# One transfer and one split per weight slot in a two-layer GLA and retention trunk

## The chip, the cores and the metric

The kernel runs on one core of one Trainium2 chip. The metric is the device time of one launch in microseconds (us). TensorE is called PE, VectorE DVE, ScalarE ACT, GpSimd POOL, SyncE SP.

## What is computed

Two layers over 2048 prompt tokens (width 1024) and over 8 single decode tokens that carry their own states. Cut to what matters:

```
def _layer(x, pos, s_gla, s_ret, norm_w, w_in, gla_w2, gla_b, ..., w_out, chunked):
    h = _rmsnorm(x, norm_w)
    z = jnp.einsum('btd,dc->btc', h, w_in).astype(F32)
    gq, gk, gv, gg, glr, rq, rk, rv, rg = _split_cols(z)
    ...
    o_a, s_gla_new = _gla_chunked(q_a, k_a, v_a, la, s_gla)
    o_b, s_ret_new = _ret_chunked(q_b, k_b, v_b, s_ret)
    ...
    mixed = jnp.concatenate([o_a, o_b], axis=-1).astype(x.dtype)
    y = x + jnp.einsum('btc,cd->btd', mixed, w_out)
    return y, s_gla_new, s_ret_new
```

All of it is float32. The two projections, h times w_in (1024 x 3088) and mixed times w_out (1024 x 1024), are most of the arithmetic.

## The kernel before

**Tiling.** The prompt is cut into 4 blocks of 512 tokens, so that 2 layers give 8 blocks, n = 0 to 7. Block b of a layer is number l * 4 + b; the decode tokens go along with the blocks b = 0 and 1 of each layer. In each block the projections are 8 units u, each 512 output columns wide: 0 to 5 from w_in, 6 and 7 from w_out. A unit is 4 slots s, and a slot is 256 rows of the weights as a tile of 128 x 1024 (two halves of 512 columns, one for each 128 rows). So there are 32 slots per block and 256 in all; w = 4u + s + 1 counts the steps of a block. Weights are read again from memory in every block.

**The split product.** A float32 product is made of three rounded ones (L754): a weight half is rounded into `w_hi` (type fp32r), the remainder goes into `w_lo`; the activations are split in the same way into `h_hi`, `h_lo` (units 0 to 5) and `m_hi`, `m_lo` (units 6 and 7). A slot is 4 banks q times 2 halves times 3 products, 24 matmuls.

**The path of a weight half.** h counts the halves (2 per slot).

- `load_half` (L244 to L258), issued from ACT's queue, brings 128 x 512 floats, 256 KB, into a staging buffer: `w_stage`, or parts of `ss` and `v_b`, which hold the decode states at other times. It waits for the last reader of that buffer. Each half has one of four semaphores `w_loaded`.
- `split_hi` (L260 to L267) on ACT waits for the load and, with the first half of a slot, for `slot_used`: the slot three before has been used by PE (RING is 3). It writes `w_hi` and raises `hi_done`.
- `split_lo` (L269 to L274) on POOL waits for `hi_done`, subtracts, writes `w_lo` and raises `lo_done`. PE waits for `lo_done` of both halves (L799 `unit_slot`), only the first slot of the program waits for each by itself (L784 `first_slot`).

In step w, ACT splits the slot w + 1 steps on and issues the load of the one behind it, half by half:

```
for h in (2 * (w + AHEAD - 1), 2 * (w + AHEAD - 1) + 1) if w > 0 else ():
    split_hi(act, n * HALVES + h)
    load_half(act, n * HALVES + h + 2)
```

**Order.** Each engine's order of work is written out by hand, step by step, and every engine works strictly in that order; semaphores tie the engines together. Around the change, these share an engine with it or stand behind it:

- ACT: `next_hi` (L366) writes `h_hi` of the next block in steps 28 to 31, right behind the step's splits; L1104 empties the low-rank product that PE's `gate_expand` (L780) needs; L1170 empties the attention outputs; the first activation of the program loads a table.
- DVE: `next_scaled` (L398) scales the next block's rows with a factor in a PSUM bank; `next_lo` (L370) writes `h_lo` from `x_t` (in the tile `xn`) and `h_hi`, both in SBUF; in step 29 four L1685 add the banks of unit 6 to the residual rows, which frees the banks for unit 7 (`free_bank` on PE). L1511 is a normalisation, L1325 updates the decode states, which PE's L873 reads.
- POOL: besides `split_lo` small powers (L627) and, at step 23, parts of `m_lo` (L687).
- PE at the start: `scale_rows` with 10 and then 18 idle turns (`idle_turns`, L375), then the first slot, with 8 idle turns behind its first product.
- SP: all other transfers; the rows of block 1 (L423) are loaded when slot 0 has been used.

Of the kernel before, what the change touches and what calls it, by code (L numbers as in the profile page):

```python
# [32 lines left out]
RING = 3  # L33
# [27 lines left out]
def build(nc, d):  # L61
# [3 lines left out]
    with ctx:  # L65
# [105 lines left out]
        w_loaded = [sem(f"w_loaded{r}") for r in range(2 * AHEAD)]  # L171
# [72 lines left out]
        def load_half(act, h):  # L244
            if h >= DEPTH * NBLK * HALVES:
                return
            before = [p for p in range(max(0, h - STAGES), h) if buffer(p) == buffer(h)]
            if before:
                act.wait_ge(lo_done, before[-1] + 1)
                if in_decode(before[-1]) and before[-1] // HALVES % NBLK == 0:  # L250
                    act.wait_ge(z_ps.sem, z_ps.at(before[-1] // HALVES // NBLK, before[-1] % HALVES // 8 + 1))
                elif in_decode(before[-1]):
                    act.wait_ge(slot_used, used(before[-1] // 2 // 4 * 4 + 3))
            elif h >= STAGES:
                act.wait_ge(state_out, h // HALVES // NBLK * 64 + 64)
                act.wait_ge(so_ps.sem, so_ps.at(h // HALVES // NBLK, 2))
            row = h // HALVES // NBLK * (SLOTS - 1) + h % HALVES // 2
            act.dma_start(stage(h), d["w_slots"][row, :, 512 * (h % 2):512 * (h % 2) + 512]).then_inc(w_loaded[h % (2 * AHEAD)], 16)  # L258

        def split_hi(act, h):  # L260
            if h >= DEPTH * NBLK * HALVES:
                return
            act.wait_ge(w_loaded[h % (2 * AHEAD)], (h // (2 * AHEAD) + 1) * 16)
            if h % 2 == 0 and h // 2 >= RING:
                act.wait_ge(slot_used, used(h // 2 - RING))
            c = slice(512 * (h % 2), 512 * (h % 2) + 512)
            nc.scalar.activation(w_hi[:, h // 2 % RING, c], stage(h), ACT.Copy).then_inc(hi_done, 1)  # L267

        def split_lo(pool, h):  # L269
            if h >= DEPTH * NBLK * HALVES:  # L270
                return
            pool.wait_ge(hi_done, h + 1)
            r, c = h // 2 % RING, slice(512 * (h % 2), 512 * (h % 2) + 512)
            pool.tensor_tensor(w_lo[:, r, c], stage(h), w_hi[:, r, c].bitcast(f32), ALU.subtract).then_inc(lo_done, 1)  # L274
# [129 lines left out]
        def _(sp):  # L404
# [109 lines left out]
            for n in range(DEPTH * NBLK):  # L514
# [8 lines left out]
                for w in range(20):  # L523
# [29 lines left out]
                    if b == 1:  # L553
                        if w == 3:
                            sp.wait_ge(lo_done, n * HALVES)
                            load_states(l, "state_ret")
                        if w == 8:
                            sp.wait_ge(stored.sem, stored.at(n, 0))
                            if l == 0:
                                sp.wait_ge(xstat.sem, xstat.at(n + 1, 1))  # L560
                            load_v(l, 0)
                        if w == 9:
                            sp.wait_ge(s_v.sem, s_v.at(l, V_SS[0]))
                            save_states(l, "ret_s")
                            load_v(l, 1)
                            sp.wait_ge(state_out, l * 64 + 32)
                            sp.wait_ge(so_ps.sem, so_ps.at(l, 1))
                            load_states(l, "state_gla")
# [44 lines left out]
        def _(pool):  # L613
# [36 lines left out]
            for h in range(2):  # L650
                split_lo(pool, h)
            for h in range(2, 2 * AHEAD):
                split_lo(pool, h)
# [3 lines left out]
            for l in range(DEPTH):  # L657
                def body(l, n, kind):
                    for w in range(SLOTS):
                        if w > 0:  # L660
                            split_lo(pool, n * HALVES + 2 * (w + AHEAD - 1))
                            split_lo(pool, n * HALVES + 2 * (w + AHEAD - 1) + 1)
# [34 lines left out]
        def _(pe):  # L697
# [10 lines left out]
            for l in range(DEPTH):  # L708
                def body(l, n, kind):
# [48 lines left out]
                    def last_slots():  # L758

                        pe.wait_ge(lo_done, DEPTH * NBLK * HALVES)  # L760
# [23 lines left out]
                    def first_slot():  # L784

                        for k in range(2):
                            pe.wait_ge(lo_done, k + 1)
                            pe.wait_ge(hlo_sb.sem, hlo_sb.at(0, k + 1))
                            products(0, 0, 0, (k,))
                            if k == 0:  # L790
                                idle_turns(pe, 8)
# [7 lines left out]
                    def unit_slot(u, s):  # L799
                        w = 4 * u + s + 1  # L800
                        first = n * HALVES + 2 * (4 * u + s)
                        pe.wait_ge(lo_done, first + 2)
# [231 lines left out]
        def _(act):  # L1034
            act.wait_ge(sets, 7)
            act.wait_ge(x_first[1], 16)
            load_half(act, 0)
            load_half(act, 1)
            act.wait_ge(first_xt[0], 16)
            load_half(act, 2)  # L1040
            load_half(act, 3)
            split_hi(act, 0)
            next_hi(act, 0, 0)
            split_hi(act, 1)
            for k in range(1, KT):
                next_hi(act, 0, k)
                if k == 1:
                    load_half(act, 4)
                    load_half(act, 5)
                if k in (2, 3):  # L1050
                    split_hi(act, k)
            for l in range(DEPTH):
                def body(l, n, kind):
# [45 lines left out]
                    for w in range(SLOTS):  # L1099
# [31 lines left out]
                        for h in (2 * (w + AHEAD - 1), 2 * (w + AHEAD - 1) + 1) if w > 0 else ():  # L1131
                            split_hi(act, n * HALVES + h)
                            load_half(act, n * HALVES + h + 2)
# [724 lines left out]
```

## Time and profile before

| what | value |
|---|---|
| median of 3 runs | 1656.39 us (1655.0 to 1656.63) |
| the profiled execution | 1656.71 us, span 1654.9 us |
| PE busy | 1636.2 us, 99% of the span |
| DVE, ACT, POOL busy | 1065.8, 616.3 and 837.1 us (64%, 37%, 51%) |
| HBM read | 219.34 MB, 161 GB/s with what is written |
| weight loads | 512 of 256 KB (344 to w_stage, 112 to ss, 56 to v_b) |

The table says that PE is nearly always at work and that every other engine has room on average. An average does not tell whether PE waits at a certain place, for that the waits and the timeline are read.

### The profile page before, as it was taken

How to read it: one execution, taken by the hardware profiler on the slowest of the kernel's cores; microseconds unless marked ns; L12 is line 12 of the kernel's file. 1: busy time of each engine (PE TensorE's matmuls, PEld its weight loads, DVE VectorE, ACT ScalarE, POOL GpSimd, SP SyncE). 2: the span in 40 equal slices, each digit the busy share in tenths (PEclk: the TensorE clock that was granted, in tenths of full speed). 3: DMA queues.
4: the chain of work that ended last, by engine and by line, in shares of the span. 5: the costliest groups of instructions: out<-in, count | busy, mean ns of one | idle time of the engine just before them, and what ended most of it. 6: DMA issues, size and time to landing. Idle time of an engine off the chain costs nothing.

```text
span 1654.9 us, 26309 instructions
## 1 busy us (share of the span) xinstructions
PE 1636.2 (99%) x9802; PEld 1353.3 (82%) x9802; DVE 1065.8 (64%) x2372; ACT 616.3 (37%) x1150; POOL 837.1 (51%) x645
## 2 busy tenths in 40 slices
PE   7999999999999999999999999999999999999998
PEld 5888878888888887888878888788888888878887
DVE  6743676678764575547854467757887557784474
ACT  4523434234342343423443234342343324442342
POOL 4543645545455454554544445456555455554455
PEclk9999999999999999999999999999999999999999
DMA  7444656767555564467643656566764377553554
GB/s 273 105 134 149 179 204 167 195 199 212 169 111 148 158 197 135 120 159 161 196 136 108 158 139 197 159 185 185 186 193 140 111 168 162 174 169 102 144 154 141
DMA packets 389135, 268.18 MB, mean 162 GB/s; under 512 B 290704, under 2 KB 293136, under 8 KB 389008
## 3 DMA queue, kind: packets, MB, share of 16 engines
q1 hardware_dynamic: 315136, 131.99, 31.4%
q10 hardware_dynamic: 73872, 134.51, 25.9%
q8 instruction: 77, 1.26, 0.3%
q14 instruction: 50, 0.41, 0.1%
HBM read 219.34 MB, written 47.07 MB: 161 GB/s over the span
## 4 chain that ended last, share of the span: by engine, by line
PE 94%; DMA 2%; DVE 2%; issue 0%; ACT 0%; SPq 0%; ACTq 0%; POOLq 0%; POOL 0%; DVEq 0%
PE bank L754 82%; PE bank L990 3%; PE bank L996 2%; DMA w_stage<-in_w_slots 2%; PE bank L974 2%; PE bank L950 2%; PE bank L839 1%; PE bank L720 1%; DVE region L1511 1%; PE bank L780 1%; PE bank L828 0%; DMA xn<-in_x_t 0%; DVE h_lo L370 0%; DVE xn L398 0%; DVE bns L1490 0%
## 5 line engine op out<-in xcount | busy, mean ns | idle before, releaser
L274 POOL TENSOR_TENSOR w_lo<-w_stage,w_hi 128x512 fp32r<-128x512 f32 x344 | 479.7, 1414 | 468.1 <-ACT w_hi L267 467.8
L754 PE MATMUL bank<-h_hi,w_hi 128*128 128x512 f32 x1024 | 407.0, 397 | 1.0 <-DVE h_lo L370 0.9
L754 PE MATMUL bank<-h_lo,w_hi 128*128 128x512 f32 x1024 | 399.1, 390 | 0.0
L754 PE MATMUL bank<-h_hi,w_lo 128*128 128x512 f32 x1024 | 398.9, 390 | 0.0
L267 ACT ACTIVATE w_hi<-w_stage 128x512 fp32r<-128x512 f32 x344 | 199.7, 624 | 490.2 <-PE bank L754 425.1
L274 POOL TENSOR_TENSOR w_lo<-ss,w_hi 128x512 fp32r<-128x512 f32 x112 | 150.5, 1361 | 165.4 <-ACT w_hi L267 165.4
L754 PEld LDWEIGHTS bank<-h_hi,w_hi 128*128 128x128 f32 x1024 | 192.1, 188 | 51.2 <-issue 6.5
L754 PEld LDWEIGHTS bank<-h_hi,w_lo 128*128 128x128 f32 x1024 | 192.2, 188 | 40.9
L754 PEld LDWEIGHTS bank<-h_lo,w_hi 128*128 128x128 f32 x1024 | 192.3, 188 | 37.4
L754 PE MATMUL bank<-w_hi,m_hi 128*128 128x512 f32 (+1 forms) x520 | 201.5, 387 | 0.0
L754 PE MATMUL bank<-w_hi,h_hi 128*128 128x512 f32 x512 | 200.9, 392 | 0.0
L754 PE MATMUL bank<-w_lo,m_hi 128*128 128x512 f32 (+1 forms) x520 | 200.8, 386 | 0.0
L754 PE MATMUL bank<-w_hi,m_lo 128*128 128x512 f32 (+1 forms) x520 | 200.6, 386 | 0.0
L754 PE MATMUL bank<-w_lo,h_hi 128*128 128x512 f32 x512 | 199.4, 389 | 0.0
L754 PE MATMUL bank<-w_hi,h_lo 128*128 128x512 f32 x512 | 199.2, 389 | 0.0
L267 ACT ACTIVATE w_hi<-ss 128x512 fp32r<-128x512 f32 x112 | 65.9, 625 | 156.5 <-PE bank L754 116.5
L627 POOL TENSOR_TENSOR rstd<-var,half 128x4 f32<-128x4 f32 x64 | 66.7, 1042 | 107.5 <-DVE var L1503 55.7
L754 PEld LDWEIGHTS bank<-w_hi,m_hi 128*128 128x128 f32 x520 | 97.6, 188 | 20.9 <-issue 1.1
L754 PEld LDWEIGHTS bank<-w_hi,m_lo 128*128 128x128 f32 x520 | 97.7, 188 | 19.8
L754 PEld LDWEIGHTS bank<-w_hi,h_hi 128*128 128x128 f32 x512 | 96.1, 188 | 21.5 <-issue 1.2
L754 PEld LDWEIGHTS bank<-w_lo,m_hi 128*128 128x128 f32 x520 | 97.7, 188 | 19.3
L754 PEld LDWEIGHTS bank<-w_hi,h_lo 128*128 128x128 f32 x512 | 96.1, 188 | 20.2
(206 smaller groups left out, 2174.9 us busy)
## 6 DMA issues: line engine op xcount, KB each, us to landing
w_stage<-in_w_slots ACTq DMA_DIRECT2D x344, 256.0 KB, 3.5
ss<-in_w_slots ACTq DMA_DIRECT2D x112, 256.0 KB, 3.9
region<-in_x_prompt SPq DMA_DIRECT2D x32, 512.0 KB, 5.0
out_o_rows<-region SPq DMA_DIRECT2D x64, 256.0 KB, 2.7
v_b<-in_w_slots ACTq DMA_DIRECT2D x56, 256.0 KB, 3.3
region<-out_o_rows SPq DMA_DIRECT2D x192, 64.0 KB, 3.1
xn<-in_x_t SPq DMA_DIRECT2D x16, 512.0 KB, 7.4
out_k_rows<-region SPq DMA_DIRECT2D x32, 256.0 KB, 3.5
```

The costliest lines, as they stand in the source:

```text
L267: nc.scalar.activation(w_hi[:, h // 2 % RING, c], stage(h), ACT.Copy).then_inc(hi_done, 1)
L274: pool.tensor_tensor(w_lo[:, r, c], stage(h), w_hi[:, r, c].bitcast(f32), ALU.subtract).then_inc(lo_done, 1)
L627: pool.tensor_tensor(dst, src, half[0:dst.shape[0], 0:dst.shape[-1]], ALU.pow).then_inc(s, 1)
L720: i = pe.matmul(ATT[r, 0:256], wg[:, k, :], x_t[:, k, 256 * hf:256 * hf + 256], start=(k < 2), stop=(k >= 6))
L754: i = pe.matmul(dst, x, y, start=(s == 0 and kk == 0 and c == 0), stop=(s == 3 and kk == 1 and c == 2), skip_group_check=True)
L780: i = pe.matmul(dst[:, 256 * p:256 * p + 256], w2b[r, 128 * p:128 * p + 128], lr_t[r, :], start=True, stop=True)
L839: i = pe.matmul(Z[Z_BANK[u]][32 * c:32 * c + 32, 0:128], hs[:, k, :], stage(first + k)[:, 128 * c:128 * c + 128], start=(k == 0), stop=(k ...
L950: i = pe.matmul((ST, X)[t // 2][r, c:c + 128], k_n[:, t, 64 * h:64 * h + 64], v_n[:, t, 128 * h:128 * h + 128], start=True, stop=True)
L974: i = pe.matmul(SC_TWO[hh][:, c:c + 128], k_t[r, p, tile], q_two[g][r, p, tile], start=True, stop=True)
L990: pe.matmul(OUT_TWO[hh][:, c:c + 128], a_two[g][:, t % 2, h, :], v_n[:, t, 128 * h:128 * h + 128], start=(t % 2 == 0 and p == 0), stop=Fal ...
L996: i = pe.matmul(OUT_TWO[hh][:, c:c + 128], q_two[g][r, p, TOK * t:TOK * t + TOK], s[r, 128 * p:128 * p + 128], start=False, stop=(t % 2 == ...
L1511: i = vec.tensor_scalar(oh, oh, agg[:, z, h, 0:1], rstd[:, z, h:h + 1], ALU.subtract, ALU.mult)
```

## The change

A slot is loaded by one transfer of 128 x 1024 floats (512 KB), rounded by one ACT instruction and subtracted by one POOL instruction of 1024 columns. `hi_done` and `lo_done` count slots instead of halves, there are two semaphores `w_loaded` instead of four, and the waits before a load are those of both halves. The matmuls, their number and order are the same.

```diff
-        w_loaded = [sem(f"w_loaded{r}") for r in range(2 * AHEAD)]
+        w_loaded = [sem(f"w_loaded{r}") for r in range(AHEAD)]
...
-        def load_half(act, h):
+        def stage_slot(h):
+            i = buffer(h)
+            if i < STAGED:
+                return w_stage[:, i:i + 2, :].rearrange("p a n -> p (a n)")
+            return ss_row[:, 512 * (i - STAGED):512 * (i - STAGED) + 1024] if i < STAGED + 4 else v_row[:, 512 * (i - STAGED - 4):512 * (i - STAGED - 4) + 1024]
+
+        def load_slot(act, h):
             if h >= DEPTH * NBLK * HALVES:
                 return
...
+            for x in (h, h + 1):
+                before = [p for p in range(max(0, x - STAGES), x) if buffer(p) == buffer(x)]
+                if before:
+                    act.wait_ge(lo_done, before[-1] // 2 + 1)
...
-            act.dma_start(stage(h), d["w_slots"][row, :, 512 * (h % 2):512 * (h % 2) + 512]).then_inc(w_loaded[h % (2 * AHEAD)], 16)
+            act.dma_start(stage_slot(h), d["w_slots"][row, :, :]).then_inc(w_loaded[h // 2 % AHEAD], 16)
 
         def split_hi(act, h):
...
-            act.wait_ge(w_loaded[h % (2 * AHEAD)], (h // (2 * AHEAD) + 1) * 16)
-            if h % 2 == 0 and h // 2 >= RING:
+            act.wait_ge(w_loaded[h // 2 % AHEAD], (h // 2 // AHEAD + 1) * 16)
+            if h // 2 >= RING:
                 act.wait_ge(slot_used, used(h // 2 - RING))
-            c = slice(512 * (h % 2), 512 * (h % 2) + 512)
-            nc.scalar.activation(w_hi[:, h // 2 % RING, c], stage(h), ACT.Copy).then_inc(hi_done, 1)
+            nc.scalar.activation(w_hi[:, h // 2 % RING, :], stage_slot(h), ACT.Copy).then_inc(hi_done, 1)
 
         def split_lo(pool, h):
...
-            pool.wait_ge(hi_done, h + 1)
-            r, c = h // 2 % RING, slice(512 * (h % 2), 512 * (h % 2) + 512)
-            pool.tensor_tensor(w_lo[:, r, c], stage(h), w_hi[:, r, c].bitcast(f32), ALU.subtract).then_inc(lo_done, 1)
+            pool.wait_ge(hi_done, h // 2 + 1)
+            r = h // 2 % RING
+            pool.tensor_tensor(w_lo[:, r, :], stage_slot(h), w_hi[:, r, :].bitcast(f32), ALU.subtract).then_inc(lo_done, 1)
...
                         for k in range(2):
-                            pe.wait_ge(lo_done, k + 1)
+                            pe.wait_ge(lo_done, 1)
                             pe.wait_ge(hlo_sb.sem, hlo_sb.at(0, k + 1))
                             products(0, 0, 0, (k,))
...
                         first = n * HALVES + 2 * (4 * u + s)
-                        pe.wait_ge(lo_done, first + 2)
+                        pe.wait_ge(lo_done, first // 2 + 1)
...
-            load_half(act, 0)
-            load_half(act, 1)
+            load_slot(act, 0)
             act.wait_ge(first_xt[0], 16)
-            load_half(act, 2)
-            load_half(act, 3)
+            load_slot(act, 2)
             split_hi(act, 0)
             next_hi(act, 0, 0)
-            split_hi(act, 1)
             for k in range(1, KT):
                 next_hi(act, 0, k)
                 if k == 1:
-                    load_half(act, 4)
-                    load_half(act, 5)
-                if k in (2, 3):
-                    split_hi(act, k)
+                    load_slot(act, 4)
+                if k == 2:
+                    split_hi(act, 2)
...
-                        for h in (2 * (w + AHEAD - 1), 2 * (w + AHEAD - 1) + 1) if w > 0 else ():
-                            split_hi(act, n * HALVES + h)
-                            load_half(act, n * HALVES + h + 2)
+                        if w > 0:
+                            h = n * HALVES + 2 * (w + AHEAD - 1)
+                            split_hi(act, h)
+                            load_slot(act, h + 2)
```

The order of instructions on ACT at the start of the program, with the semaphores each waits for. Before:

```order
L258 DMA w_stage<-in_w_slots 128x512 [waits x_first1,sets]
L258 DMA w_stage<-in_w_slots 128x512
L258 DMA w_stage<-in_w_slots 128x512 [waits first_xt0]
L258 DMA w_stage<-in_w_slots 128x512
L267 ACT_TABLE_LOAD
L267 ACTIVATE w_hi<-w_stage 128x512 [waits w_loaded0]
L366 ACTIVATE h_hi<-xn 128x512 [waits h_sb,nw_in]
L267 ACTIVATE w_hi<-w_stage 128x512 [waits w_loaded1]
L366 ACTIVATE h_hi<-xn 128x512 [waits h_sb]
L258 DMA w_stage<-in_w_slots 128x512 x2
```

And of the change:

```order
L265 DMA w_stage<-in_w_slots 128x1024 [waits x_first1,sets]
L265 DMA w_stage<-in_w_slots 128x1024 [waits first_xt0]
L273 ACT_TABLE_LOAD
L273 ACTIVATE w_hi<-w_stage 128x1024 [waits w_loaded0]
L372 ACTIVATE h_hi<-xn 128x512 [waits h_sb,nw_in]
L372 ACTIVATE h_hi<-xn 128x512 [waits h_sb]
L265 DMA w_stage<-in_w_slots 128x1024
```

The first `h_hi` now stands behind the rounding of the whole slot 0, not of its first half. The lines shift: L258, L267, L274, L366 and L370 of before are L265, L273, L280, L372 and L376.

## Rows read from the trace of the kernel before

**Rows 1.** The page, part 1: busy us (share of the span) and instructions of each engine

```profile
PE 1636.2 (99%) x9802; PEld 1353.3 (82%) x9802; DVE 1065.8 (64%) x2372; ACT 616.3 (37%) x1150; POOL 837.1 (51%) x645
```

**Rows 2.** Waits of PE: who waited for whom, us in total, times, longest

```profile
PE bank L754 <- DVE h_lo L370: 0.9, 1, 0.9
PE bank L873 <- DVE ss L1325: 0.9, 1, 0.9
PE bank L780 <- ACT region L1104: 0.9, 1, 0.9
```

**Rows 3.** Groups by line: out<-in, shapes, xcount | busy us, mean ns | idle before

```profile
L274 POOL TENSOR_TENSOR w_lo<-w_stage,w_hi 128x512 fp32r<-128x512 f32 x344 | 479.7, 1414 | 468.1 <-ACT w_hi L267 467.8
L1195 ACT ACTIVATE region<-region,yrs 128x1024 f32<-128x1024 f32 x3 | 3.5, 1151 | 13.1 <-POOL yrs L627 13.1
```

**Rows 4.** Timeline, end of block 0: start us, us, engine, line [idle before <-releaser]

```profile
204.16 0.63 ACT L267 ACTIVATE w_hi<-ss 128x512 fp32r<-128x512 f32 x1 [3.56 <-PE bank L754]
204.86 1.29 POOL L274 TENSOR_TENSOR w_lo<-ss,w_hi 128x512 fp32r<-128x512 f32 x1 [2.89 <-ACT w_hi L267]
205.86 0.85 DVE L370 TENSOR_TENSOR h_lo<-xn,h_hi 128x512 fp32r<-128x512 f32 x1 [2.46 <-ACT h_hi L366]
206.11 1.75 POOL L274 TENSOR_TENSOR w_lo<-ss,w_hi 128x512 fp32r<-128x512 f32 x1
206.63 1.78 DVE L370 TENSOR_TENSOR h_lo<-xn,h_hi 128x512 fp32r<-128x512 f32 x1
208.34 2.47 DVE L1685 TENSOR_TENSOR region<-bank,region 128x512 f32<-128x512 f32 x4
209.34 0.40 PE L754 MATMUL bank<-w_hi,m_hi 128*128 128x512 f32 x1
```

**Rows 5.** Timeline, the start of the program

```profile
9.91 2.34 PE L375 MATMUL bank<-ident 128*128 128x128 f32 x10
11.41 0.46 ACTq L258 DMA_DIRECT2D w_stage<-in_w_slots  x1
11.90 1.28 ACT L267 ACT_TABLE_LOAD   x1 [11.90 <-DMA xn<-in_x_t]
12.53 2.41 PE L375 MATMUL bank<-ident 128*128 128x128 f32 x18
13.90 2.97 POOL L274 TENSOR_TENSOR w_lo<-w_stage,w_hi 128x512 fp32r<-128x512 f32 x2 [1.92 <-ACT w_hi L267]
14.38 1.35 DVE L370 TENSOR_TENSOR h_lo<-xn,h_hi 128x512 fp32r<-128x512 f32 x1
15.88 0.47 PE L754 MATMUL bank<-h_hi,w_hi 128*128 128x512 f32 x1 [0.94 <-DVE h_lo L370]
17.57 0.47 PE L754 MATMUL bank<-h_hi,w_hi 128*128 128x512 f32 x1
19.82 0.69 DVE L370 TENSOR_TENSOR h_lo<-xn,h_hi 128x512 fp32r<-128x512 f32 x1
```

**Rows 6.** Timeline, two more block ends (blocks 6 and 3)

```profile
1424.61 2.55 DVE L370 TENSOR_TENSOR h_lo<-xn,h_hi 128x512 fp32r<-128x512 f32 x2 [2.27 <-ACT h_hi L366]
811.18 2.48 DVE L1685 TENSOR_TENSOR region<-bank,region 128x512 f32<-128x512 f32 x4 [0.15 <-DMA region<-in_x_prompt]
812.92 2.56 POOL L274 TENSOR_TENSOR w_lo<-ss,w_hi 128x512 fp32r<-128x512 f32 x2 [2.44 <-ACT w_hi L267]
```

**Rows 7.** The page, part 6: DMA issues, KB each, median us from issue to landing

```profile
w_stage<-in_w_slots ACTq DMA_DIRECT2D x344, 256.0 KB, 3.5
...
region<-in_x_prompt SPq DMA_DIRECT2D x32, 512.0 KB, 5.0
```

**Rows 8.** Timeline, block 1 of layer 0

```profile
304.83 0.63 ACT L267 ACTIVATE w_hi<-w_stage 128x512 fp32r<-128x512 f32 x1 [3.65 <-DMA w_stage<-in_w_slots]
319.95 6.76 DVE L1511 TENSOR_SCALAR region<-region,agg,rstd 128x128 f32<-128x128 f32 x8
331.49 2.31 DVE L1325 TENSOR_TENSOR ss<-ss,v_b 128x1024 f32<-128x1024 f32 x1
```

More of the change, by code:

```diff
@@ L242, in in_decode @@
             return kind == 0 and j <= 24 or kind == 1 and j > 24
-        def load_half(act, h):
+        def stage_slot(h):
[4 more added lines that the diff above has]
+        def load_slot(act, h):
             if h >= DEPTH * NBLK * HALVES:
                 return
[L247 to L256, printed above, removed]
+            for x in (h, h + 1):
+                before = [p for p in range(max(0, x - STAGES), x) if buffer(p) == buffer(x)]
+                if before:
+                    act.wait_ge(lo_done, before[-1] // 2 + 1)
+                    if in_decode(before[-1]) and before[-1] // HALVES % NBLK == 0:
+                        act.wait_ge(z_ps.sem, z_ps.at(before[-1] // HALVES // NBLK, before[-1] % HALVES // 8 + 1))
+                    elif in_decode(before[-1]):
+                        act.wait_ge(slot_used, used(before[-1] // 2 // 4 * 4 + 3))
+                elif x >= STAGES:
+                    act.wait_ge(state_out, x // HALVES // NBLK * 64 + 64)
+                    act.wait_ge(so_ps.sem, so_ps.at(x // HALVES // NBLK, 2))
             row = h // HALVES // NBLK * (SLOTS - 1) + h % HALVES // 2
-            act.dma_start(stage(h), d["w_slots"][row, :, 512 * (h % 2):512 * (h % 2) + 512]).then_inc(w_loaded[h % (2 * AHEAD)], 16)
+            act.dma_start(stage_slot(h), d["w_slots"][row, :, :]).then_inc(w_loaded[h // 2 % AHEAD], 16)
         def split_hi(act, h):
@@ L554, in _ @@
                         if w == 3:
-                            sp.wait_ge(lo_done, n * HALVES)
+                            sp.wait_ge(lo_done, n * HALVES // 2)
                             load_states(l, "state_ret")
@@ L649, in _ @@
                 rsqrt(xrs[:, 2 * g:2 * g + 2], xvar[:, 2 * g:2 * g + 2], first_rs)
[L650 to L653, printed above, removed]
+            split_lo(pool, 0)
+            split_lo(pool, 2)
             pool.wait_ge(s_v.sem, s_v.at(0, V_NV - V_LAST))
@@ L661, in body @@
                             split_lo(pool, n * HALVES + 2 * (w + AHEAD - 1))
-                            split_lo(pool, n * HALVES + 2 * (w + AHEAD - 1) + 1)
                         if w == 16 and n % NBLK == 2:
@@ L758, in last_slots @@
                     def last_slots():
-                        pe.wait_ge(lo_done, DEPTH * NBLK * HALVES)
+                        pe.wait_ge(lo_done, DEPTH * NBLK * HALVES // 2)
                         for q in range(3):
```

## The prediction, as it stood before the result

> **What bounds the kernel now.** I read the page first: TensorE (PE) is busy for 99% of the span [rows 1]. A microsecond taken off ACT, POOL, DVE or a transfer is worth nothing by itself; only what makes PE wait counts, and what PE loses it does not get back. The waits of PE come next: behind its first constant it has three, of 0.9 us each [rows 2]. In the groups by line stands the changed work: POOL's remainder takes 1.41 us on average [rows 3], ACT's rounding 0.63 [rows 4]. It is done well ahead. For 252 slots I compared the end of the second remainder with the slot's first matmul: the median lead is 8.5 us, and behind the first three slots none is under 2.5. Weights as such don't bind.
>
> What binds is POOL against DVE. At a block's end POOL works on a first half for 1.29 us and then takes 1.75 us for the second, and DVE's h_lo (L370) takes 0.85 and then 1.78 us [rows 4], though 0.69 with POOL idle [rows 5]. One reading fits the ends: the first h_lo, ready at 205.86, waits for POOL's first half (end 206.15) and needs 0.55 more; POOL's second half waits for that h_lo (206.71), ends at 207.86, and the second h_lo ends 0.55 later. Each is shut out for the other's whole instruction. DVE instructions that read a PSUM bank are not: L1685 takes 2.48 us for four in block 3, two of them beside POOL, and 2.47 without [rows 4, 6].
>
> Behind the h_lo stand the four L1685 that empty the banks of unit 6. The first is done near 209.02 (208.34 and a quarter of the group, with 0.07 of overlap) and PE's next group starts at 209.34 [rows 4]: 0.32 us is all the slack of the block end. The same picture, to 0.01 us, stands at four more (blocks 2, 3, 4 and 6; one of them in rows 6); in block 3 L1685 waits for a transfer until 811.18 [rows 6].
>
> **The change, part by part.**
>
> (a) *Loads.* 512 issues of 256 KB become 256 of 512 KB. An issue holds ACT's queue for some 0.4 us, mostly beside ACT's own work, so fewer of them save nothing, but at the start: there the second issue of slot 1 (0.46 us) stands before the table load [rows 5]. A load of 256 KB lands after 3.5 us in the median, one of 512 KB of another kind after 5.0 [rows 7]: 1.5 us more, covered by the leads; if they were gone, PE would pay it in each slot. Cost 0, bounds -0.5 and +1.
>
> (b) *Rounding.* Two halves, started 0.54 apart, end 1.15 us after the start; one instruction of 1024 columns takes 1.15 us in another line [rows 3]. Same end, but POOL can't begin after the first half: 0.5 us later.
>
> (c) *Remainder.* Two back to back take 2.56 us [rows 6]; one of 1024 columns, by the slope, the same. The time in which DVE is shut out stays, but it is one piece into which nothing gets, and it starts 0.5 us late. No row here shows a POOL instruction of 2.5 us with DVE waiting; I take the whole length, since the waits of rows 4 end where POOL's halves end. If no wait were longer than those show (1.3 us), (d) would be 0 and the sum near 2.5. The Trainium skill, SBUF — State Buffer, section "SBUF: two separate sides", calls this port pair an exclusive lock that the first comer holds for the whole instruction; by it the sum is the one below.
>
> (d) *Block ends.* ACT starts at 204.16 [rows 4] and ends at 205.31; POOL follows 0.07 later, as now, and ends at 207.92. h_lo, ready at 205.86, comes 0.48 us too late: it ends at 208.47, the next at 209.07, and L1685 starts at 208.99 for 208.34. Of the 0.65 us the slack takes 0.32: PE waits 0.35 (0.5 in block 3). Five block ends: 1.9 us; bounds 0 (DVE comes first) and 3.3 (no slack).
>
> (e) *Start.* PE's first product now needs both halves. ACT can round between 12.7 (0.5 earlier) and 14.3 (there it begins the second half now, without a wait); 13.5 is the middle, as the loads queue behind the first inputs. End 14.65; POOL from 14.7 to 17.25, now 13.90 to 16.87; h_lo, ready at 15.2, ends at 17.8, now 15.73 [rows 5]. PE starts at 17.95 for 15.88. Then L398 (0.66 us) and h_lo give 19.15 for PE's second product, for 17.57 [rows 5]: 1.6 us. The next slot's remainder shuts out its rows' h_lo once more, some 0.2. What follows is as late: the loads of the next block's rows start when slot 0 is done, the load of slot 3 stands behind them, and its rounding of 1.15 us stands ahead of L1104, for which PE already waits 0.9 us [rows 2]: 0.2 more. 2.0 us; bounds 0.5 and 3.5.
>
> (f) *Block 1 of layer 0.* PE waits 0.9 us for L1325 [rows 2], which took 2.31 us because one of POOL's halves had begun [rows 8]; one piece adds 1.25. Before it eight L1511 of 0.33 us take 6.76 us [rows 8]: after each POOL instruction one gets in, and with three long ones for five some 1.1 us is lost. At 304.83 the rounding had waited 3.65 us for a load, with L1170 and this chain of DVE behind it [rows 8]: both halves now count, 0.5 us more or less. Sum 2.35, of which I take 2.0; bounds 0 and 3.5. In layer 1 PE doesn't wait there, and the lead is some 3 us: 0.
>
> (g) *The rest.* By the same comparison, DVE's other deliveries lead PE by over 1.7 us, which 0.65 doesn't reach: 0, bound +1.
>
> Sum: 2.0 + 1.9 + 2.0 = 5.9 us. The profiled execution took 1656.71 us (span 1654.9), 0.3 above the median of the runs shown, 1656.39. On the median: 1662.3.
>
> **The rivals.**
>
> *Little reaches PE (no change).* For it: 99% busy and the long leads. Against it: slack of 0.32 us, five times. It needs DVE to come first at the block ends: the margin is 0.48 us, so it decides if a rounding of 1024 columns takes over 1.6 us instead of 1.15, or if DVE gets into a long POOL instruction. Then (d) is 0, (f) under 1, (e) is left: some 2 us, 1658.5.
>
> *Not slower, but faster.* The saved issue brings the rounding to 12.7, POOL and DVE hand over half as often, and PE's three waits go. Price 3 x 0.9 = 2.7 us [rows 2]: 1653.7. It decides only if slot 0 has landed by 12.7 and DVE comes first at all three.
>
> *The clock.* Ten idle turns took 2.34 us and the next 18 only 2.41 [rows 5]: half rate at first, then full. The gap between them and PE's first product, 0.94 us [rows 5], becomes 3.0. If the clock falls from 2.4 to 1.2 GHz in it, PE's first products run at half rate; at the start that lasted at least from 9.91 to 12.25 [rows 5]. I take 3 us, of which half is lost: 1.5 us, 1663.8. The Trainium skill, TensorE: Matmul & The Clock Gate, part 1, says that an idle PE is put back to half rate; no row here shows such a fall.
>
> *Loads bind.* If the whole slot comes 2 to 3 us after the time of its first half where SP crowds the queues, as at 304.83 [rows 8], then the smallest leads (2.5 to 4 us, block 5) go and L1170 is late for PE: 3 us more, 1665.3.
>
> **How the numbers follow.** Forecast 0.48; clock on top 0.14; loads on top 0.11; little reaches PE 0.23; faster 0.04. About 0.2%, 3.3 us, is what a measurement of this kernel can tell from no change: 1653.1 to 1659.7. Slower: 0.48 + 0.14 + 0.11, less 0.02 for my sum's lower bounds, 0.71. Faster by over 0.2% needs more than the three waits: 0.02. Same 0.27. The range goes from 1657.8, which takes in most of "little reaches PE", to 1666.5, above both upper rivals; each side leaves about 1 in 10.
>
> **What would show it.** Right: a remainder near 2.55 us; at five block ends a first h_lo of 2.6 us and a wait of PE for L1685 of 0.3 to 0.5; PE's first product near 18; a wait for L1325 of over 2 us. Wrong: an h_lo of 0.7 us beside the long POOL instruction; PE's waits still three of 0.9; a granted clock under 1 behind the first products. Wrong in kind: PE's new waits are for w_lo, not for DVE.

## The result, and the profile after

The changed kernel takes 1662.55 us (median of 6 runs, 1660.21 to 1664.17), the kernel before 1656.5 (6 runs, 1654.9 to 1658.02): ratio 1.0038, 95% interval 1.0026 to 1.005. It is slower by over 0.2%, as forecast, and the median lies 0.25 us from the predicted 1662.3. The profiled execution took 1663.84 us (span 1662.0), 7.1 us more than that of before.

The page, part 1 and part 5 (busy us and mean ns), against [rows 1] and [rows 3]:

```profile
PE 1639.7 (99%) x9802; PEld 1356.1 (82%) x9802; DVE 1110.4 (67%) x2372; ACT 588.9 (35%) x894; POOL 754.6 (45%) x389
...
L280 POOL TENSOR_TENSOR w_lo<-w_stage,w_hi 128x1024 fp32r<-128x1024 f32 x172 | 421.3, 2449 | 540.9 <-ACT w_hi L273 540.9
...
L273 ACT ACTIVATE w_hi<-w_stage 128x1024 fp32r<-128x1024 f32 x172 | 182.0, 1058 | 513.3 <-PE bank L757 404.7
```

POOL loses 82.5 us of work and ACT 27.4, and DVE is busy 44.6 us longer with the same 2372 instructions. The time in which it is shut out counts as busy, as in the h_lo of 2.43 us below.

The waits of PE, against [rows 2]:

```profile
PE bank L993 <- DVE s_at L1471: 1.8, 1, 1.8
PE bank L783 <- ACT region L1103: 1.7, 1, 1.7
PE bank L757 <- DVE region L1685: 1.6, 1, 1.6
PE bank L757 <- DVE h_lo L376: 1.3, 1, 1.3
```

The wait for L1325 is gone. It is gone from the other traces too, but for 0.2 us in one, so it belongs more to the one traced execution of the kernel before than to that kernel; more on this under (f). To place the 7.1 us I subtracted, matmul by matmul, the start times of the 6168 weight products of the two traces. The difference is flat but for a few steps (each step is the growth of the delay since the row above):

| where | start before | start after | step |
|---|---|---|---|
| first product | 15.88 | 16.89 | +1.01 |
| slot 1 | 22.98 | 23.56 | -0.43 |
| behind gate_expand, block 0 | 34.85 | 36.16 | +0.73 |
| end of block 0 (unit 7) | 209.34 | 210.90 | +0.25 |
| block 1, behind the reads of s_at | 301.43 | 306.75 | +3.76 |
| block 1, behind the decode states | 334.94 | 339.28 | -0.98 |
| end of block 2 | 613.82 | 618.44 | +0.28 |
| end of block 3 | 812.02 | 818.45 | +1.81 |
| end of block 4 | 1024.57 | 1031.27 | +0.27 |
| end of block 6 | 1428.09 | 1435.13 | +0.34 |

The start of the program, against [rows 5]:

```profile
12.70 1.06 ACT L273 ACTIVATE w_hi<-w_stage 128x1024 fp32r<-128x1024 f32 x1 [1.04 <-DMA w_stage<-in_w_slots]
...
13.84 2.35 POOL L280 TENSOR_TENSOR w_lo<-w_stage,w_hi 128x1024 fp32r<-128x1024 f32 x1 [2.09 <-ACT w_hi L273]
...
14.31 2.43 DVE L376 TENSOR_TENSOR h_lo<-xn,h_hi 128x512 fp32r<-128x512 f32 x1 [0.31 <-ACT h_hi L372]
...
16.89 0.47 PE L757 MATMUL bank<-h_hi,w_hi 128*128 128x512 f32 x1 [1.33 <-DVE h_lo L376]
```

h_lo is ready at 14.31 and ends 0.55 us behind POOL's end (16.19): nothing gets into the long instruction. The end of block 3, against [rows 6]:

```profile
813.01 1.06 ACT L273 ACTIVATE w_hi<-ss 128x1024 fp32r<-128x1024 f32 x1 [3.25 <-DMA ss<-in_w_slots]
...
814.15 2.40 POOL L280 TENSOR_TENSOR w_lo<-ss,w_hi 128x1024 fp32r<-128x1024 f32 x1 [2.39 <-ACT w_hi L273]
814.63 3.07 DVE L376 TENSOR_TENSOR h_lo<-xn,h_hi 128x512 fp32r<-128x512 f32 x2 [2.06 <-ACT h_hi L372]
817.63 2.47 DVE L1685 TENSOR_TENSOR region<-bank,region 128x512 f32<-128x512 f32 x4
818.45 0.47 PE L757 MATMUL bank<-w_hi,m_hi 128*128 128x512 f32 x1 [1.62 <-DVE region L1685]
```

The forecast chain stands there, and at its head the rounding waited for the slot's load, which added 1.5 us at this end and in this execution alone.

Block 1 holds the largest step. DVE and SP in it, in the timeline (L1579 is the last instruction of each of DVE's rotary chains, there are four such chains, and SP stores k's rows behind them; the first two lines are of the kernel before):

```profile
258.12 1.66 DVE L1579 TENSOR_TENSOR region<-region,tmp 128x512 f32<-128x512 f32 x1
259.87 3.44 SPq L458 DMA_DIRECT2D out_k_rows<-region  x2
```

and after:

```profile
259.75 2.40 POOL L280 TENSOR_TENSOR w_lo<-w_stage,w_hi 128x1024 fp32r<-128x1024 f32 x1 [3.46 <-ACT w_hi L273]
259.77 2.92 DVE L1579 TENSOR_TENSOR region<-region,tmp 128x512 f32<-128x512 f32 x1
262.78 5.46 SPq L464 DMA_DIRECT2D out_k_rows<-region  x2
269.93 8.97 SPq L469 DMA_DIRECT2D k_n<-out_k_rows  x16
280.03 0.33 ACTq L265 DMA_DIRECT2D w_stage<-in_w_slots  x1
280.20 1.24 SPq L505 DMA_DIRECT2D v_b<-out_v_s  x2
...
295.06 1.23 DVE L1303 TENSOR_TENSOR region<-region,k_s 128x1024 f32<-128x1024 f32 x1 [10.09 <-DMA v_b<-out_v_s]
...
301.21 3.63 PE L993 MATMUL bank<-region,tmp 128*128 128x128 f32 x16 [1.83 <-DVE s_at L1471]
```

Three of the four L1579 meet a POOL instruction of 2.4 us and take 2.77 to 2.92 us. The two stores of k's rows take 5.46 us from the first issue to the end of the second, not 3.44, and SP's queue with v_b in it moves 3.5 us back, where PE is only 1.7 us later. v_b then lands some 14 us after its issue (before: 276.66 to 283.05), DVE idles 10.09 us for it, and PE waits 1.83 us.

How late v_b is goes with one thing more, the order of two issues. Here ACT's queue issues the load of a slot at 280.03, just ahead of the two reads of v_b. In the trace of e2, an experiment of the next section with the remainder in halves, it goes out behind them:

```profile
281.52 1.24 SPq L531 DMA_DIRECT2D v_b<-out_v_s  x2
282.51 0.34 ACTq L271 DMA_DIRECT2D w_stage<-in_w_slots  x1
```

There the second read is issued later than here (282.16 for 280.84) and lands earlier (289.37 for 295.04). It is so in all fourteen traces: in the six with a step in block 1 the load is issued 0.15 to 0.9 us ahead of v_b's first read, and the second read lands 12.8 to 14.2 us after its issue; in the eight without a step no load stands just ahead, and it takes 5.4 to 7.2 us. No experiment moved this load by itself, so the order is a strong suspect and not a shown cause.

The same 16 matmuls take 2.02 us in another trace of this kernel and 3.63 here. The windows view, with the granted clock in the third column from the end, says why:

```profile
295.00:300.00 5.00, 4.38 (x20) 3.30 (x18) 4.87 (x9) 1.06 (x1) 2.01 (x1) 1.00 0.46 132
300.00:305.00 5.00, 3.79 (x20) 3.60 (x22) 4.96 (x6) 1.06 (x1) 3.35 (x2) 0.66 0.36 108
305.00:310.00 5.00, 5.00 (x46) 4.33 (x45) 3.60 (x16) 1.08 (x2) 0.36 (x1) 1.00 0.73 254
```

The clock fell from 2.4 to 1.2 GHz behind the wait, for 1.6 us more on PE.

### The profile page after: what moved, and what is told of

It is laid out like the page before. It is cut to its first block, busy times and chain, and to the rows that moved or that the text cites. A ratio compares the mean times of both kernels' runs of the same rounds, so it can differ in the third digit from the quotient of the medians.

```text
span 1662.0 us, 25711 instructions
## 1 busy us (share of the span) xinstructions
PE 1639.7 (99%) x9802; PEld 1356.1 (82%) x9802; DVE 1110.4 (67%) x2372; ACT 588.9 (35%) x894; POOL 754.6 (45%) x389
## 4 chain that ended last, share of the span: by engine, by line
PE 95%; DMA 2%; DVE 2%; SPq 1%; issue 0%; ACT 0%; POOLq 0%; POOL 0%; DVEq 0%; ACTq 0%
PE bank L757 82%; PE bank L993 4%; PE bank L999 2%; PE bank L977 2%; PE bank L953 2%; PE bank L842 1%; DMA v_b<-out_v_s 1%; DMA w_stage<-in_w_slots 1%; PE bank L723 1%; PE bank L783 1%; SPq L469 1%; DVE h_lo L376 0%; PE bank L831 0%; DVE region L1579 0%; DMA region<-in_x_prompt 0%
## 5 line engine op out<-in xcount | busy, mean ns | idle before, releaser
L280 POOL TENSOR_TENSOR w_lo<-w_stage,w_hi 128x1024 fp32r<-128x1024 f32 x172 | 421.3, 2449 | 540.9 <-ACT w_hi L273 540.9
L273 ACT ACTIVATE w_hi<-w_stage 128x1024 fp32r<-128x1024 f32 x172 | 182.0, 1058 | 513.3 <-PE bank L757 404.7
L280 POOL TENSOR_TENSOR w_lo<-ss,w_hi 128x1024 fp32r<-128x1024 f32 x56 | 135.0, 2412 | 185.5 <-ACT w_hi L273 185.5
L273 ACT ACTIVATE w_hi<-ss 128x1024 fp32r<-128x1024 f32 x56 | 59.2, 1057 | 153.6 <-PE bank L757 90.5
L757 PEld LDWEIGHTS bank<-w_lo,h_hi 128*128 128x128 f32 x512 | 96.2, 188 | 19.4
```

What stands on the lines that cost most here:

```text
L273: nc.scalar.activation(w_hi[:, h // 2 % RING, :], stage_slot(h), ACT.Copy).then_inc(hi_done, 1)
L280: pool.tensor_tensor(w_lo[:, r, :], stage_slot(h), w_hi[:, r, :].bitcast(f32), ALU.subtract).then_inc(lo_done, 1)
L757: i = pe.matmul(dst, x, y, start=(s == 0 and kk == 0 and c == 0), stop=(s == 3 and kk == 1 and c == 2), skip_group_check=True)
```

## The experiments

They ran in four groups on three chips, and beside each group the kernel before ran on the same chip, where it took 1655.2 to 1655.3 us; ratios are to it. I began from two theories: the *length* of POOL's instruction shuts DVE out, or the *late start* behind the whole rounding does it; with the *load* as a rival.

**The changed kernel once more** (e0, no edit).

> The changed kernel again, beside the three others on one chip: 1662.5 us within 1.5. Its six runs lay in two groups (1660.2 to 1661.3 and 1663.8 to 1664.2). If the difference between these is a collision of transfers in block 1 (a v_b load of 14.2 us in the profiled execution), a profile of the lower group shows a step of PE near 301 us smaller by 2 to 4 us and the same steps elsewhere.

Measured: 1660.91 us (6 runs, 1658.35 to 1662.81), ratio 1.0033 (1.0021 to 1.0044). The step in block 1 is +0.95 (PE waits 0.62 us for s_at, clock 1.00) and in block 3 +0.29. Start +1.56, the five block ends 1.65 in all. That makes 3.2 us against the trace of the kernel before. But that trace has the wait for L1325 (-0.98), which no other trace has, but for 0.2 us in e3; without it the cost in this execution is 4.2 us, and by the time of the run it is 4.6 (1659.94 against the median of 1655.31 beside it). v_b landed as long after its issue as in the first trace (13.0 us for 14.2), so the theory on record, a collision that is missing here, did not hold. PE waited 0.62 us for 1.83, and its clock stayed at 1.00; the step of block 3 shrank as well. The rest of the cost comes and goes: of the twelve runs of the changed kernel six have a mean clock of 0.999 (1658.35 to 1661.25) and six of 0.998 or 0.997 (1661.14 to 1664.17).

**Whole loads alone** (e1).

```diff
+ if h % 2 == 0:
+     act.dma_start(stage_slot(h), d["w_slots"][row, :, :]).then_inc(w_loaded[h // 2 % AHEAD], 16)
```

> Whole slots are loaded, rounding and remainder stay in halves of 512 columns. If POOL's long hold of the port makes the loss: the kernel is back at the time of before, 1656.5 us within 1 us; the five block ends keep h_lo of 0.85 and 1.78 us and PE doesn't wait for L1685; PE's first product comes up to 0.5 us earlier than at 15.88, since one issue less stands before the table load. If the loads make it (rival): PE's step near 301 to 306 us in block 1 and the one of block 3's end stay, 1659 to 1661 us.

Measured: 1657.18 us (11 runs), ratio 1.0011 (1.0002 to 1.002). The first product comes 0.43 us earlier than before, and then it is lost again in one place:

```profile
32.57 0.63 ACT L294 ACTIVATE w_hi<-w_stage 128x512 fp32r<-128x512 f32 x1 [5.64 <-DMA w_stage<-in_w_slots]
...
33.63 0.46 ACT L1136 ACTIVATE region<-bank,bias_row 128x256 f32<-128x256 f32 x1
```

```profile
30.00:35.00 5.00, 2.91 (x29) 2.10 (x26) 2.60 (x5) 1.51 (x3) 1.72 (x2) 1.00 0.42 137
35.00:40.00 5.00, 5.00 (x18) 3.81 (x15) 4.13 (x11) 3.99 (x8) 3.31 (x3) 0.66 0.40 127
```

L1136 (L1104 of before) stands behind the rounding of slot 3, that waited 5.64 us for its load, PE waited 2.1 us, and the clock fell (0.66 in the window). In this place the whole load is not free. Elsewhere it is: there is no step in block 1 nor at the block ends, so the rival "the loads bind there" failed. The theory that put this kernel back at the time of before, within 1 us, missed by the 1.9 us lost at this place.

**Loads and roundings whole, remainders in halves** (e2).

```diff
+ nc.scalar.activation(w_hi[:, h // 2 % RING, :], stage_slot(h), ACT.Copy).then_inc(hi_done, 2)
```

> Loads and the rounding on ACT whole, the remainder on POOL in halves, so that POOL starts 0.5 us later but holds the port for 1.3 us at a time. If the late start makes the loss at the block ends: both h_lo end where they do in the changed kernel, since POOL and DVE still share the port one after the other, and PE waits 0.2 to 0.35 us for L1685 at five block ends; the start improves (first product before 16.9). If the length makes it: no wait for L1685. Time by the first 1658 to 1660 us, by the second 1656.5 to 1657.5.

Measured: 1661.11 us (6 runs), ratio 1.0033 (1.0021 to 1.0046). Block ends +0.28, +0.30, +0.56, +0.27 and +0.36, as in the changed kernel; no step at 301. The block ends bear out the late start; the start did not improve (the first product came at 17.08, not before 16.9), and the time lies above both forecasts. Most of the delay (3.8 of the 4.6 us in the trace) is there by slot 2 and says little of the theories: in this build ACT's table load ran behind the slot's landing (12.70), not ahead of it, PE waited 2.4 us for the low-rank copy, and the clock fell.

**Remainders whole, loads and roundings in halves** (e3).

```diff
+ pool.wait_ge(hi_done, h + 2)
+ pool.tensor_tensor(w_lo[:, r, :], stage_slot(h), w_hi[:, r, :].bitcast(f32), ALU.subtract).then_inc(lo_done, 2)
```

> Loads and rounding in halves as before, only POOL's remainder is one instruction of 1024 columns, which waits for both halves. If POOL's one long piece (its length and its later start) makes the loss: 1661 to 1663 us, as in the changed kernel, with PE's first product at 16.9 or later, five waits for L1685 and DVE's L1579 of 2.8 to 2.9 us. If the loads take part: 1659 us or less, with block 1 losing under 1.5 us.

Measured: 1661.17 us (5 runs), ratio 1.0034 (1.0021 to 1.0048). Block ends +0.43, +0.42, +0.49, +0.44 and +0.50. Either part alone makes a block end late, and the two don't add up: both theories hold there, and the three parts can't be priced by subtraction. The clock fell here too, behind a wait of 1.80 us at gate_expand, which cost 1.6 us of low rate.

The step of block 1 is missing, and L1579 takes 0.69 us, where 2.8 to 2.9 had been expected:

```profile
261.71 0.69 DVE L1611 TENSOR_TENSOR region<-region,tmp 128x512 f32<-128x512 f32 x1
261.82 2.84 POOL L302 TENSOR_TENSOR w_lo<-w_stage,w_hi 128x1024 fp32r<-128x1024 f32 x1 [3.46 <-ACT w_hi L294]
```

(L1611 is L1579.) Here DVE begins 0.11 us ahead of POOL, in the changed kernel 0.02 us behind it. The long remainder alone does not make the step: a tenth of a microsecond decides who waits.

**ScalarE's queue at gate_expand** (g1). In the changed kernel:

```diff
+ if n == 0 and w == 3:
+     slot_work(2)
+ if w > 0 and (n > 0 or w != 2):
+     slot_work(w)
```

> The changed kernel with one step reordered: in block 0 ScalarE copies lr_t (L1103 of the changed kernel) ahead of the rounding of slot 3, not behind it, so the copy no longer waits for that slot's load. Theory A (a good part of the start's cost is this queue: PE idle 1.75 us in front of gate_expand, the slot's load landed at 33.60 and the rounding of 1.06 us ran ahead of the copy): PE's wait in front of gate_expand falls to 0.4 to 0.7 us, the start's delay against the kernel before falls from 1.3 to about 0.1 to 0.4 us, and since this wait is long enough for the clock to fall in some executions, which costs 1.5 us more in those, the median falls by 1 to 2 us against the changed kernel (1660.9 on this chip, so 1659 to 1660). Theory B (the slot is late, not the copy): the rounding of slot 3 behind the copy is late for PE's next slot and the wait comes back there, median as the changed kernel within 0.5.

Measured: 1669.51 us (5 runs, 1666.43 to 1673.78), ratio 1.0085 (1.007 to 1.01). Both theories missed. The wait at gate_expand went (PE is there at 34.14, 0.7 us before the old kernel), and 10.3 us were lost at slot 9:

```profile
PE bank L953 <- DVE k_n L1444: 8.8, 1, 8.8
```

```profile
64.37 7.85 SPq L469 DMA_DIRECT2D k_n<-out_k_rows  x16
...
71.42 0.34 ACTq L265 DMA_DIRECT2D w_stage<-in_w_slots  x1
...
81.34 1.25 DVE L1437 STREAM_TRANSPOSE k_n<-k_n 128x1024 f32<-128x1024 f32 x1 [11.89 <-DMA k_n<-out_k_rows]
```

The sixteen reads of k_n, each 32 KB, are issued until 72.2; the load of slot 11, 512 KB, is issued at 71.42, ahead of the last of them (71.77), and this one lands at 81.3, with the load itself (ACT rounds at 81.00). In the trace of the changed kernel the reads were out at 70.8 and the load at 72.93, and k_n was there at 72.94. The edit brought PE 2 us and the load 1.5 us forward, but not DVE and SP.

**h_hi ahead of the weights' rounding at the block ends** (g2). In the changed kernel:

```diff
+ if 28 <= w < 32 and n < LAST:
+     next_hi(act, n + 1, 2 * (w - 28))
+     next_hi(act, n + 1, 2 * (w - 28) + 1)
  slot_work(w)
```

> The changed kernel with one step reordered: in the last four slots of each block but the last, ScalarE rounds the next block's activations (h_hi) ahead of the slot's weights, not behind them. VectorE's remainder h_lo can then start before GpSimd's remainder of the weights. Theory A (the block ends cost because POOL's one instruction of 2.4 us shuts h_lo out, and L1685 behind it is late for PE): h_lo pieces take 0.68 instead of 2.4 us, PE's wait for L1685 goes, the five or six block-end steps of 0.25 to 0.35 us (1.8 in one block where the load bound) disappear or turn negative, and the median falls by 1.5 to 3 us against the changed kernel (to 1658 to 1659.5 on this chip). Theory B (the ends are late because the rounding of the weights itself ends late, at the load): the slot's rounding comes no earlier, the w_lo pieces come 1.2 us later at each end, and the time stays or rises.

Measured: 1659.48 us (11 runs), ratio 1.0022 (1.0013 to 1.0031), 1.4 us under the changed kernel on another chip, which is less than these intervals can tell; the trace tells it. All five steps at the block ends are gone. The end of block 3 (L1688 is L1685):

```profile
808.63 1.28 DVE L376 TENSOR_TENSOR h_lo<-xn,h_hi 128x512 fp32r<-128x512 f32 x2
...
810.23 2.41 POOL L280 TENSOR_TENSOR w_lo<-ss,w_hi 128x1024 fp32r<-128x1024 f32 x1 [2.33 <-ACT w_hi L273]
813.11 2.48 DVE L1688 TENSOR_TENSOR region<-bank,region 128x512 f32<-128x512 f32 x4 [3.20 <-DMA region<-in_x_prompt]
```

Two h_lo take 1.28 us, not 3.07, and DVE idles before L1688. So (d) is shown: it was this order that made the ends late.

**Both moves in the kernel before** (g3).

> The kernel before (halves everywhere) with both reorderings: the lr_t copy ahead of slot 3's rounding in block 0, and h_hi ahead of the weights' rounding in the last four slots of a block. By theory A for both it gains little at the start (its wait there was 0.90 us and 0.4 to 0.6 remain, so 0.2 to 0.4) and at the block ends what stands there between the last product of a block and the first of the next beyond the switch (at most 0.3 us each, seven times): 1653 to 1655 against 1655.3. By theory B no difference or slower.

Measured: 1654.11 us (11 runs), ratio 0.9991 (0.9983 to 1.0). The gain is at gate_expand (-0.98); at the block ends there was nothing to win. The trace also lacks the wait for L1325, but so do the traces without the moves, and it is no gain of theirs.

**Both moves with whole loads, splits in halves** (g4).

> Loads of 512 KB, roundings and remainders in halves (the part of the change that cost 1.9 us by itself), with both reorderings. Where that cost was PE's 2.1 us wait for the lr_t copy and the low clock after it (0.85 instead of 0.46 us for two products over 3.4 us), it goes: 1653 to 1655 against 1655.3 for the kernel before, that is 2 to 4 us under the same kernel without the reorderings (1657.2). If whole loads cost by binding slots elsewhere, it stays at 1656.5 to 1657.5.

Measured: 1654.11 us (11 runs), ratio 0.9992 (0.9983 to 1.0001), 3.1 us under the same kernel without the moves and level with the last one. Where the moves are made, whole loads cost nothing. Both kernels lie some 1.2 us under the kernel before, less than the 0.2% that a measurement here can tell.

**Remainder in halves again** in the changed kernel (h1).

```diff
+ pool.tensor_tensor(w_lo[:, r, 0:512], stage_slot(h)[:, 0:512], w_hi[:, r, 0:512].bitcast(f32), ALU.subtract)
+ pool.tensor_tensor(w_lo[:, r, 512:1024], stage_slot(h)[:, 512:1024], w_hi[:, r, 512:1024].bitcast(f32), ALU.subtract).then_inc(lo_done, 1)
```

> The changed kernel with GpSimd's remainder in two instructions of 512 columns again (load and rounding stay whole). Theory A (the length of GpSimd's one instruction is what shuts VectorE's rotary multiplications out, so that the two row stores of k stand 5.46 us apart instead of 3.44, k_n comes late, and PE waits in block 1): the stores stand 3.4 to 3.5 us apart again, the step of the delay in block 1 goes to 0 to 0.3 us, and h_lo at the start takes 1.3 and not 2.4 us, so that the first product comes 1.0 us earlier against the changed kernel; the block-end steps stay at 0.25 to 0.35 each, since the rounding of 1.06 us still ends late there. Median 1657.5 to 1659.5 on this chip (changed kernel 1660.9). Theory B (the late start behind the whole rounding is what costs): no gain, 1660.5 to 1661.5.

Measured: 1660.24 us (6 runs), ratio 1.0029 (1.0018 to 1.004). The two stores of k's rows take 3.45 us again and block 1 has no step, as theory A says; the time lies between the forecasts of A and B. The start it had wrong: the first product comes at 16.80, since now POOL's second half is shut out by h_lo (1.72 us) and PE needs both; and the wait at gate_expand was 2.1 us with a fallen clock in the profiled run. The length alone is worth little while the rest stands.

**Changed kernel, both moves** (h2).

> The changed kernel with both reorderings (lr_t copy ahead of slot 3's rounding, h_hi ahead of the weights' at the block ends). Theory A (what the first reordering alone did, 8.6 us slower, came from the last of the sixteen reads of k_n in block 0 being issued behind a slot's load, 71.77 against 71.42 us, and landing only at 81.3): PE again runs ahead of SyncE's chain, and PE waits some 8 us in front of k_n's products near 80 us in most executions: 1664 to 1668. Theory B (a chance arrangement of that one build): 1657 to 1659.

Measured: 1662.74 us (10 runs) in two groups: five from 1657.43 to 1659.41, as theory B has it, five from 1666.06 to 1668.9, as theory A has it. The profiled run is of the lower group: last reads of k_n issued by 73.2, load of slot 11 at 71.43, k_n there at 75.94, PE's wait 1.8 us. There is no trace of the upper group.

So being issued behind the load is not enough to be 9 us late: here three reads are, and they land with it, but the load lands after 3.9 us (75.33), in g1 after 9.6 (80.98). What differs is how soon SP's four stores of f_rows follow: from 73.20 here, from 72.26 in g1. In the other traces with whole loads, the load issued next to these stores takes 9.5 to 12.5 us. The runs don't separate the part of the stores from that of the order.

**Changed kernel, remainders in halves, both moves** (h3).

> The changed kernel with the remainder in halves and both reorderings. Theory A (the cliff at 80 us belongs to the long remainder, which delays the row stores of k by 2 us, and the block ends and the start to the two places in ScalarE's queue): no wait in front of k_n's products, no step at the block ends, 1653.5 to 1655, level with the kernel before (1655.3) or up to 1.5 us under it. Theory B (the whole rounding costs by itself): 1656 to 1658.

Measured: 1655.0 us (11 runs, 1654.59 to 1656.37), ratio 0.9999 (0.9991 to 1.0008). Level with the kernel before, as theory A has it: with whole loads and whole roundings, and without the length and the two places in the queue, nothing of the cost is left against it; against the kernel before with the moves 0.9 us are.

**The load held behind the keys** (i1), in the kernel of both moves (h2):

```diff
  split_hi(act, h)
+ if n == 0 and v == 9:
+     act.wait_ge(kb_in.sem, kb_in.at(0, 256))
  load_slot(act, h + 2)
```

> The changed kernel with both reorderings, as in h2, and one wait more: in block 0 ScalarE issues the load of slot 11 (at 71.43 us in h2) only when the sixteen reads of k_n have landed. h2 fell into two groups, five executions at 1657.4 to 1659.4 and five at 1666.1 to 1668.9. Theory A (the slow group is the one in which the last reads of k_n are caught behind that load and land some 9 us late): no execution above 1662, median 1657.5 to 1660, PE's wait in front of k_n's products 0 to 0.5 us; the load goes 2 to 3 us later and its slot, first used some 18 us behind, does not miss it. Theory B (the slow group has another cause, such as f_rows or the store of v ahead of the load): two groups again, or PE waits for slot 11 instead.

Measured: 1656.92 us (11 runs, 1655.86 to 1658.09), ratio 1.0008 (0.9999 to 1.0017). No second group, and no wait for k_n. The load of slot 11 went out at 72.38, 0.95 us later than in h2:

```profile
71.45 1.05 ACT L273 ACTIVATE w_hi<-w_stage 128x1024 fp32r<-128x1024 f32 x1
72.38 0.33 ACTq L265 DMA_DIRECT2D w_stage<-in_w_slots  x1
```

The median is 5.8 us lower, but in h2 it lay in the gap between the groups; what the wait took away is some 9 us in half of the executions. In this one the reads were out early (70.7), so the hold was short. The time lies a little under theory A's range (1657.5 to 1660), and its main sign is there, no execution above 1662: with the load behind the reads the upper group is gone. That the reads were caught behind the load in that group is inferred from this and from g1's trace.

## Why the prediction was right

*The sum.* Forecast 5.9 us; measured 6.05 on the medians of the first runs and 5.6 in the repetition. The traces give 7.1 (after) and 3.2 (the same kernel again), or 8.1 and 4.2 without the wait for L1325 that the trace of before has. So the forecast was right in direction, and at the block ends in mechanism, but that it hit the median within 0.25 us is luck: some 4 us are in both traces, and up to 4 more come and go with the execution (the fastest of twelve ran 3.0 us above the kernel before), where the forecast had 5.9 steady ones. Of its three terms, (d) held, (e) was over, and (f) came by another path.

*(a) Loads, 0.* Mis-sized: 1.9 us by themselves (0.3 to 3.3 by the interval). I had given 0.2 us to the load of slot 3 ahead of L1104, and that place is worth 0.7 us in the changed kernel and, with the clock, 2.6 in the kernel with whole loads alone. The 0.5 us gained at the start was there (-0.43).

*(b), (c) Rounding and remainder.* The instructions are shorter than the neighbouring line and the slope said: 1.06 us for 1.15, 2.35 to 2.45 for 2.56. That DVE gets in nowhere was right where POOL came first: h_lo took 2.43 us.

*(d) Block ends, 1.9.* Right in place, chain and size: four of five steps are 0.25 to 0.34 for the 0.35 forecast, 1.65 in all in the second trace. In block 3 the profiled run lost 1.81 for 0.5, since the rounding waited for its load: the rival "loads bind", in one place and some executions.

*(e) Start, 2.0.* Direction right, size over: +1.31 and +1.56. The failed step is "13.5 is the middle": the slot landed at 12.70, the early bound, so PE started at 16.89 and not at 17.95. That, too, is of the execution: in g2, with the same start, the slot landed at 13.50 and PE started at 17.70, and 2.2 us were lost by gate_expand. Behind it, gate_expand cost 0.73 for the 0.2 I gave it.

*(f) Block 1, 2.0 through L1325.* It came to +2.8 in the profiled run and to 0.0 in the second trace, within the bounds of 0 and 3.5, but the path was wrong. L1325 did grow by the length, from 2.31 to 3.42 us, as forecast (3.56). But the 0.9 us wait on which this was built is, by all signs, an accident of the one trace of that kernel (1656.71 us, where the median beside the later runs is 1655.3). There the rounding at 304.83 had waited 3.65 us for its load [rows 8], L1170 stood behind it, and DVE's chain behind L1170 began at 306.47; in the kernel of g3, also in halves, at 302.05:

```profile
306.47 0.87 DVE L1490 BATCH_NORM_STATS2 bns<-region 128x6 f32<-128x128 f32 x4 [3.63 <-ACT region L1170]
302.05 0.86 DVE L1496 BATCH_NORM_STATS2 bns<-region 128x6 f32<-128x128 f32 x4
```

Against PE, this chain begins 3.5 to 3.7 us earlier in the thirteen other traces than in that of before, and L1325 has room for its 1.1 us more (PE waits 0.2 us for it in e3, and in no other).

What did cost is the rotary chain and with it SP's queue, which (g) had put at 0 by leads over 1.7 us: those leads were read for DVE's deliveries in their present order, and did not count what DVE holds up in SP's queue. Halving POOL's instruction in the changed kernel takes the step away (h1), so the length is needed for it; it is not enough (e3), since POOL must also come first. How much PE then loses changes from run to run.

*Rivals.* The clock (0.14) came true, not behind the first product, where PE waited up to 3.0 us with the clock at 1.00 behind it, but at gate_expand, in block 1 or at slot 9, and it cost about the 1.5 us forecast: 1.5 to 1.6 each time it fell behind a wait of 1.8 to 2.4 us. The Trainium skill, TensorE: Matmul & The Clock Gate, part 1, says that an idle PE is put back to half rate; the traces agree in six kernels, at these three places, and disagree after 3.04 us at the start. "Loads bind" (0.11) came true at one block end of one execution, 1.5 us at the end of block 3. "Faster" is ruled out. "Little reaches PE" needed DVE to come first at the block ends, and in both traces POOL did; by time alone it was not far off, since the fastest of the twelve runs (1658.35) lies 3 us above the kernel before.

*The lock.* The Trainium skill, SBUF — State Buffer, section "SBUF: two separate sides", says that the first comer holds the port pair for the whole instruction. The trace agrees at 2.4 us: POOL 13.84 to 16.19, h_lo from 14.31 to 16.74.

## What to carry to other kernels

Before a transfer or an instruction is merged, look for what stands behind it in the queue of its engine: the copy behind slot 3's rounding and the h_hi behind the weights cost PE 0.7 and 1.6 us in the changed kernel, while the instructions saved gave it nothing. Putting the small urgent work ahead of the large patient one gave this back, but with the long remainder it brought a new loss in half of the executions (h2); only with the remainder in halves again (h3) was the kernel level with the one before. A long POOL instruction was as long a hole for the DVE instructions with two SBUF inputs that came behind it (h_lo, L1579, L1325); look beyond DVE, into the queue that waits for DVE. A wait that stands in a single trace may be of that execution: see it in a second one before a forecast is built on it. And moving PE forward is not safe by itself: if its loads move forward and another engine's chain does not, a large transfer can get among the small reads that PE needs first.

## What the runs showed of the hardware

- Reads of 32 KB with a load of 512 KB issued ahead of the last of them landed 9.1 us behind the last issue (g1: 72.22 to 81.3), where it takes 2.1 in the changed kernel (70.8 to 72.9) and 2.8 in the lower group of h2. One and the same program (h2) fell into two groups of executions, 9 us apart, and did not once the load was held (i1).
- A load of 512 KB takes 9.5 to 12.5 us when it is issued next to SP's four stores of f_rows, and 3.3 to 5.3 in the steps before, in the eleven traces with whole loads.
- The clock fell at PE waits of 1.80, 1.83, 2.09, 2.14, 2.38 and 8.8 us and not at 1.72, 1.74, 1.75 and 1.77 us, and neither at 1.82 to 3.04 us at the start. By the length of the wait alone it can't be told.
- A remainder of 1024 columns takes 2.35 us with nothing in its way, two of 512 columns 2.56; a rounding of 1024 takes 1.06 us, two of 512 columns 1.15.
- POOL and DVE take turns by who begins first, and a difference of 0.02 us is enough (POOL 259.75, DVE 259.77: DVE's 0.69 us become 2.92; DVE 261.71, POOL 261.82: POOL's 2.40 become 2.84).
